# Weights loaded in pieces over the unit before, keys projected a block ahead, and the first layer's transposes on TensorE

## The chip, the cores and the metric

The kernel runs on the 8 cores of one Trainium2 chip. Every core works on one sequence of the batch, with the same weights, and the cores exchange nothing. The metric is the device time of the slowest core in microseconds.

## The reference: what is computed

A trunk of four pre-norm residual layers over a sequence of 16 meta tokens and 2048 tokens, model width 1024, branch width 2048. Layers 0 and 2 are pooling mixers, layers 1 and 3 are gated linear attention (GLA); a final RMSNorm follows, and the meta positions are dropped.

- Pooling layer: `u, z = split(h @ w_in)`. The 2048 channels of u fall into four groups of 512 with trailing windows of 2, 4, 8 and 16 tokens; from the mean over the window the token itself is subtracted, a 512 x 512 matrix of the group follows, then a channel scale and `silu(z)`, and `@ w_out` is added to h.
- GLA layer: four heads, key width 256, value width 512. `log_a = log_sigmoid(glr @ w_gate2 + b) / 16`, where `glr` is a projection of rank 16 of the normed input. Over chunks, with `cum` the running sum of `log_a`: `o = tril(qe ke^T) v + qe S` with `qe = q exp(cum)`, `ke = k exp(-cum)`, and the state `S = exp(g) S + kd^T v`. Then an RMSNorm per head, `silu(z)`, and `@ w_out` is added to h.

## The kernel before, in words

**Layout.** h stays in SBUF in float32 for the whole run (16 tiles of 128 tokens by 1024, and the meta tokens apart). The normed activations stand transposed in `hnT` (features on partitions, bfloat16). `BLOCKS` cuts the tokens into nine blocks: 144 tokens, seven of 256, 128 (two tiles of 128 in a block of 256).

**Units.** The work is 16 units: four groups per pooling layer (windows 8, 16, 4, 2 in this order) and four heads per GLA layer. Each unit goes over the nine blocks. A unit has four weight buffers, `W[0]` to `W[3]`, of 128 x 4096 bfloat16, in two sets (`Wt[0]`, `Wt[1]`) that alternate from unit to unit. `wload` (L462) fills one by a DMA from POOL's queue, which reads 2 MB of float32 and casts it. `load_unit(ui)` (L483) issues all loads of a unit; it is called at the end of a unit for the unit after the next (L719, L907), so each load waits on POOL's queue for the last reader of the buffer it fills.

**Pooling unit** (`pool_layer`, L605). `fold(ui)` (L506) multiplies the group matrix into the weights of u: 32 matmuls of 512 columns, in which ACT copies the results to `W[0]`. It is called in the unit before, after block 4 (for unit 0, at its own start), and behind it the output weights are loaded over the group matrix in `W[2]`. Per block: `zpart` and `upart` (32 matmuls each of the block's columns), `window` (prefix sums on POOL, then VectorE), `outp` (16 matmuls of 512 columns, added to h).

**GLA unit** (`gla_layer`, L731). Per block `proj` (L766) makes q, k, v and z, `gates` (L743) the decays of the next block, and `chunk` (L824) runs once per tile: scores, output, state update, output projection. The state update needs `kd`, which is `ke` transposed by a DMA from SP's queue (`xbar`, L407), issued in `proj` as soon as `ke` is written; there are two `kd` buffers. `glr_block` (L570) makes the rank-16 projection of a block from `hnT`, 8 matmuls, in the last unit of the pooling layer, right behind the block's `outp` (`after_block`, L593).

**Norms.** `norm_tile` (L552): ACT squares and sums (`rms`), VectorE scales into one of two buffers `hnb`, and a DMA transpose from SP's queue writes `hnT`. In layer 0 `norm_block` (L563) does so at the start of unit 0, two blocks ahead; later `after_tile` (L583) does it behind the last output projection of a tile.

**Order.** No order is written out. `Prog.schedule` (L109) takes all operations with their dependences and planned costs and simulates five in-order queues (PE, ACT, DVE, POOL, SP); whatever is ready first goes first, ties by the order of the program. The planned costs are constants: an operation of PE counts as ready 200 ns late (`PE_SLACK`), a VectorE operation costs `n/0.96 + 68` ns, one of POOL `1.7 n + 100` ns, a DMA 2200 ns and its bytes at 200 B/ns. DMAs have three planned channels (`bulk`, `x`, `tr`) that don't disturb each other in the plan. The result is a fixed order per queue, and `place` adds the semaphore waits. A DMA whose waits aren't met holds up everything behind it on the queue that issues it, ACT and POOL included: the loads of x are issued from ACT's queue (L916), each waiting for the one two before it.

**Start.** `load_first` (L470) loads the group matrix, the two halves of Wu (`W[3]`), then the z and the output weights of unit 0; `load_unit(1)` follows.

Of the kernel before, what the change touches and what calls it, by code (L numbers as in the profile page):

```python
# [41 lines left out]
class Prog:  # L42
# [3 lines left out]
    SEM = 120.0  # L46
    PE_SLACK = 200.0
    DMA_NS_PER_BYTE = 1.0 / 200.0
    DMA_FIX = 2200.0

    def __init__(self):
        self.ops = []
        self.dsems = {}

    def _touch(self, op, reads, writes):
# [227 lines left out]
def tile_col0(i):  # L283
    return 0 if i == 0 else NMETA + (i - 1) * 128
# [9 lines left out]
def build(n_layers=4):  # L294
# [60 lines left out]
    def carve(phase, name, nbytes, dtype, shape):  # L355
# [8 lines left out]
                 ("SA", 4352, F32, [128, 4, 272]), ("sg1", 2048, F32, [128, 2, 256]), ("U0", 4352, F32, [128, 4, 272]),  # L364
                 ("Y0", 2048, BF16, [128, 4, 256]), ("Y1", 2048, BF16, [128, 4, 256]), ("Y2", 2048, BF16, [128, 4, 256])]
    plan_gla = [("Eq", 2048, F32, [128, 2, 256]), ("Ek", 2048, F32, [128, 2, 256]),
                ("el0", 32, F32, [128, 2, 2]), ("el1", 32, F32, [128, 2, 2]), ("el2", 32, F32, [128, 2, 2]),
                ("qe0", 1024, BF16, [128, 2, 256]), ("ke0", 1024, BF16, [128, 2, 2, 128]),
# [6 lines left out]
                ("sz1", 2048, BF16, [128, 4, 256]),  # L375
                ("kd1", 512, BF16, [128, 256]), ("am1", 256, BF16, [128, 128]),
                ("S", 4096, F32, [128, 2, 512]), ("Sb", 2048, BF16, [128, 2, 512]),
# [17 lines left out]
    def mm(reads, writes, lst):  # L395
# [9 lines left out]
        P.op("pe", fn, reads, writes, dur, 170.0)  # L405

    def xbar(sem, out_, in_, reads, writes, nbytes):  # L407
        P.dma("sp", sem, lambda q: q.dma_start_transpose(out=out_, in_=in_), reads, writes, nbytes, chan="tr")  # L408
# [16 lines left out]
    def dve_dur(n):  # L425
        return n / 0.96 + 68.0

# [33 lines left out]

    def wload(ui, p, c0, c1, dst, name, part=None):  # L462
        s = ui % 2
        b = Wb[s][p] if part is None else part
        return dma("pool", name, dst, wpack[ui][:, c0:c1], [], [b], 128 * (c1 - c0) * 4)

# [15 lines left out]

    def load_unit(ui):  # L483
        if ui >= len(units):
            return
        li, u = units[ui]
        s = ui % 2
        W = Wt[s]
        if li % 2 == 0:
            wload(ui, 1, 4096, 8192, W[1][:], "W%d1" % s)  # L490
            wload(ui, 3, 12288, 16384, W[3][:], "W%d3" % s)
            wg_at[ui] = (W[2][:, 0:2048], Wb[s][2])
            dma("pool", "W%d2" % s, W[2][:, 0:2048], wpack[ui][:, 0:2048], [], [Wb[s][2]], 128 * 8192)
        else:
            for p in range(4):
                wload(ui, p, 4096 * p, 4096 * p + 4096, W[p][:], "W%d%d" % (s, p))

# [8 lines left out]
    def fold(ui):  # L506

        s = ui % 2
        W = Wt[s]
        wg, wgb = wg_at[ui]  # L510
        WuT = W[3][:, :].rearrange("p (fc n) -> p fc n", fc=4)
        wgv = wg.rearrange("p (fc n) -> p fc n", fc=4)
        for mt in range(8):
            b = proj_bank()
            mm([Wb[s][3], wgb] + ([b_wuh[mt // 4]] if ui == 0 else []), [bank[b]],
               [(PS[b][:, :], WuT[:, fc, mt * 128:(mt + 1) * 128], wgv[:, fc, :], fc == 0, fc == 3) for fc in range(4)])
            act([bank[b]], [Wb[s][0]], W[0][:, mt * 512:(mt + 1) * 512], PS[b][:, :], AF.Copy, psum=True)
        if ui != 0:
            wload(ui, 2, 8192, 12288, W[2][:], "W%d2" % s)

# [26 lines left out]
    def rms(i, k):  # L547
        act([hb[i]], [b_hnb[k], b_stat[i]], hnb[k][:, :], h[:, i - 1, :], AF.Square, accum=ssb[:, i:i + 1])
        act([b_stat[i], b_eps], [b_stat[i]], rstd[:, i:i + 1], ssb[:, i:i + 1], AF.Ln, scale=1.0 / D, bias=epsc[:, 0:1])
        act([b_stat[i]], [b_stat[i]], rstd[:, i:i + 1], rstd[:, i:i + 1], AF.Exp, scale=-0.5)  # L550

    def norm_tile(i):  # L552
# [39 lines left out]

    def after_block(li, bi):  # L593
        if li + 1 < n_layers and (li + 1) % 2 == 1:
            glr_block(bi, 4)

    orot = [0]
# [7 lines left out]
    def pool_layer(li, ui0):  # L605
# [3 lines left out]
        for gi in order:  # L609
# [7 lines left out]
            Wo = W[2][:, :].rearrange("p (oc n) -> p oc n", oc=4)  # L617
            for bi in range(NB):
                tiles, c0, n = BLOCKS[bi]
                if li == 0 and gi == 0:  # L620
# [77 lines left out]
                if ui == 0:  # L698
                    if bi == 0:
                        fold(0)  # L700
                    upart()
                    if bi == 0:
                        dma("pool", "cst2", tri[:], cst[:, 128:256], [], [b_tri], 65536, after=[xs[9]])
                        load_unit(1)
                    zpart()
# [25 lines left out]
    def gla_layer(li, ui0):  # L731
# [11 lines left out]
        def gates(k_):  # L743
            hd, bi = steps[k_]
            tiles, c0, n = BLOCKS[bi]
            el, b_el = T["el%d" % (k_ % 3)], A["el%d" % (k_ % 3)]
            offs = offs_of(bi)
# [17 lines left out]

        def proj(k_):  # L766
            hd, bi = steps[k_]
            ui = ui0 + hd
            s = ui % 2
# [3 lines left out]
            Wv = W[1][:, :].rearrange("p (kc n) -> p kc n", kc=8)  # L773
            Wz = W[2][:, :].rearrange("p (kc n) -> p kc n", kc=8)
            tiles, c0, n = BLOCKS[bi]
            par = k_ % 2
            rd = [hnTb[t_] for t_ in tiles]
            qe, ke, sz = T["qe%d" % par], T["ke%d" % par], T["sz%d" % par]
            b_qe, b_ke, b_sz = A["qe%d" % par], A["ke%d" % par], A["sz%d" % par]
            for dst, bd, Wm in ((qe, b_qe, Wq), (ke, b_ke, Wk)):  # L780
                b = proj_bank()
# [6 lines left out]
                else:  # L788
# [7 lines left out]
                    for k, (t_, o, m) in enumerate(offs_of(bi)):  # L796
                        if t_ < NT - 1:
                            kn = "kd%d" % (t_ % 2)
                            xbar(kn, T[kn][:, :].rearrange("p (f m) -> p f m", f=2), ke[:, k, :, :].rearrange("p f m -> p (f m)"),
                                 [b_ke], [A[kn]], 65536)  # L800
            for t_, o, m in offs_of(bi):
# [22 lines left out]
        def chunk(k_, k, t_, o, m):  # L824
# [5 lines left out]
            b_qe, b_ke, b_sz = A["qe%d" % par], A["ke%d" % par], A["sz%d" % par]  # L830
            el, b_el = T["el%d" % (k_ % 3)], A["el%d" % (k_ % 3)]
            vn = "vb%d" % (t_ % 3)
            vb = T[vn]
            cp = t_ % 2
            kdn, amn, yn, rn = "kd%d" % cp, "am%d" % cp, "yT%d" % cp, "rs%d" % cp
            kd, am, yT, rs = T[kdn], T[amn], T[yn], T[rn]
# [53 lines left out]

        nproj[0] = 3
        gates(0)
        for k_, (hd, bi) in enumerate(steps):
            ui = ui0 + hd
            proj(k_)
            if k_ + 1 < len(steps):
                gates(k_ + 1)
            for k, (t_, o, m) in enumerate(offs_of(bi)):
                chunk(k_, k, t_, o, m)
            if hd == 3:  # L900
                after_block(li, bi)
# [4 lines left out]
            if bi == NB - 1:  # L906
                load_unit(ui + 2)  # L907
                if hd < 2:
                    load_wg2(j, hd + 2)
# [90 lines left out]
```

How the kernel before makes its waits and increments, by code:

```python
        def replay(e, h):  # L233
            for waits, o in self.q[e]:
                for k, v in waits.items():
                    h.wait_ge(esem[k] if k in esem else dsem[k], v)
                ins = o.fn(h)
                if ins is None:
                    continue
                if o.sem is not None:
                    ins.then_inc(dsem[o.sem], 16)
                else:
                    ins.then_inc(esem[e], 1)
```

## Time and profile before

| | us |
|---|---|
| median of 3 runs | 2097.07 |
| lowest, highest | 2091.41, 2119.79 |
| profiled execution | 2109.36 |
| its span, slowest core (2) | 2107.8 |
| spans of the eight cores | 2047.6 to 2107.8 |
| PE busy on core 2 | 1899.1 |
| DVE, ACT, POOL busy | 1337.8, 1262.5, 441.9 |

All rows are of core 2 unless they say otherwise. PE is TensorE's matmuls, PEld its weight loads, which overlap them. Time is counted from the first instruction. `PEclk` is the clock that TensorE was granted in a stretch, 1.00 being 2.4 GHz and 0.50 1.2 GHz. A DMA has an issue on a queue (POOLq, SPq, ACTq) and a time to landing.

### The profile page before, as it was taken

How to read it: one execution, taken by the hardware profiler on the slowest of the kernel's cores; microseconds unless marked ns; L12 is line 12 of the kernel's file. 1: busy time of each engine (PE TensorE's matmuls, PEld its weight loads, DVE VectorE, ACT ScalarE, POOL GpSimd, SP SyncE). 2: the span in 40 equal slices, each digit the busy share in tenths (PEclk: the TensorE clock that was granted, in tenths of full speed). 3: DMA queues.
4: the chain of work that ended last, by engine and by line, in shares of the span. 5: the costliest groups of instructions: out<-in, count | busy, mean ns of one | idle time of the engine just before them, and what ended most of it. 6: DMA issues, size and time to landing. Idle time of an engine off the chain costs nothing.

```text
span 2107.8 us, 45126 instructions; the slowest of 8 cores (2047.6 to 2107.8 us)
## 1 busy us (share of the span) xinstructions
PE 1899.1 (90%) x15726; PEld 1353.8 (64%) x15944; DVE 1337.8 (63%) x2159; ACT 1262.5 (60%) x2711; POOL 441.9 (21%) x468
## 2 busy tenths in 40 slices
PE   1399989996998999999899998999799899899997
PEld 0267667774765766766566766777466576666765
DVE  0185555785775776777675556578466567677787
ACT  1365455564665665667675554556455566666786
POOL 1156683321000000000014667322000000000000
PEclk7699999998999999999999999999788899999999
DMA  9954122325004004022444221232500600500111
GB/s 166 121 115 78 30 42 41 67 48 105 10 10 87 9 15 83 9 43 42 75 69 55 51 41 31 41 71 46 100 7 8 86 9 10 88 9 9 39 70 75
DMA packets 121904, 111.15 MB, mean 53 GB/s; under 512 B 106944, under 2 KB 108880, under 8 KB 114640
## 3 DMA queue, kind: packets, MB, share of 16 engines
q0 software_dynamic: 11328, 63.49, 17.7%
q1 hardware_dynamic: 108048, 36.37, 9.4%
q10 hardware_dynamic: 2304, 8.39, 1.4%
q8 instruction: 130, 2.13, 0.4%
q14 instruction: 94, 0.77, 0.1%
HBM read 138.15 MB, written 8.39 MB: 70 GB/s over the span
## 4 chain that ended last, share of the span: by engine, by line
PE 71%; DMA 10%; issue 6%; DVE 5%; ACT 4%; POOL 3%; SPq 0%; ACTq 0%; DVEq 0%; POOLq 0%
PE ps L403 71%; DMA hnT<-hnb 6%; DMA kd<-ke 3%; POOL SA L434 2%; DVE hnb L429 1%; ACT sg L423 1%; POOL SB L434 1%; DVE Y L434 1%; ACT hnb L423 1%; DMA gbc<-gains 1%; DVE h L434 1%; DVE h L429 1%; ACT rstd L423 0%; ACT U L423 0%; SPq L408 0%
## 5 line engine op out<-in xcount | busy, mean ns | idle before, releaser
L403 PE MATMUL ps<-hnT,W 128*128 128x256 bf16 (+1 forms) x9216 | 994.5, 265 | 34.1 <-ACT U L423 28.3
L403 PEld LDWEIGHTS ps<-hnT,W 128*128 128x128 bf16 x9216 | 836.0, 99 | 184.2 <-issue 45.6
L429 DVE SCALAR_TENSOR_TENSOR h<-ps,rs,h 128x512 f32<-128x512 f32 x256 | 191.7, 749 | 132.0 <-ACT rs L423 59.8
L403 PE MATMUL ps<-W,Y 128*128 128x512 bf16 x957 | 240.8, 389 | 35.4 <-DVE Y L434 26.3
L403 PE MATMUL ps<-W,hnT 128*128 128x512 bf16 x1028 | 251.2, 386 | 6.6 <-DVE Eq L758 2.7
L434 DVE TENSOR_TENSOR h<-h,ps 128x512 f32<-128x512 f32 x256 | 175.2, 684 | 123.5 <-PE ps L403 121.9
L439 POOL COPY el<-Eq 128x2 f32<-128x2 f32 x136 | 27.5, 202 | 1013.5 <-ACT Eq L423 873.5
L403 PE MATMUL ps<-W,yT 128*128 128x512 bf16 x954 | 233.9, 385 | 4.4
L423 ACT ACTIVATE Sb<-S,el 128x512 bf16<-128x512 f32 x256 | 183.7, 717 | 65.5 <-DVE S L429 37.1
L429 DVE SCALAR_TENSOR_TENSOR S<-S,el,ps 128x512 f32<-128x512 f32 x240 | 178.4, 743 | 61.7 <-PE ps L403 47.5
L434 POOL TENSOR_TENSOR SA<-U 128x1080 f32<-128x1080 f32 (+7 forms) x72 | 134.8, 1872 | 332.6 <-ACT U L423 213.6
L423 ACT ACTIVATE U<-ps,vec 128x256 f32<-128x256 f32 (+2 forms) x288 | 129.2, 449 | 112.8 <-PE ps L403 86.4
L403 PEld LDWEIGHTS ps<-W,Y 128*128 128x128 bf16 x1024 | 98.9, 100 | 130.6 <-issue 43.9
L423 ACT ACTIVATE sg<-sg 128x512 f32<-128x512 f32 (+2 forms) x288 | 168.0, 585 | 21.6 <-ACT sg L423 1.1
L403 PEld LDWEIGHTS ps<-W,hnT 128*128 128x128 bf16 x1088 | 104.9, 99 | 110.6 <-issue 20.4
L423 ACT ACTIVATE gs<-gs 128x512 f32<-128x512 f32 (+2 forms) x288 | 168.0, 583 | 7.9 <-ACT gs L423 0.4
L429 DVE SCALAR_TENSOR_TENSOR hnb<-h,rstd,gbc 128x1024 bf16<-128x1024 f32 x64 | 105.5, 1649 | 102.3 <-ACT rstd L423 93.6
L423 ACT ACTIVATE hnb<-h 128x1024 bf16<-128x1024 f32 x80 | 84.3, 1054 | 138.1 <-DMA hnT<-hnb 85.7
L429 DVE SCALAR_TENSOR_TENSOR sz<-ps,vec,gs 128x256 bf16<-128x256 f32 (+2 forms) x288 | 129.9, 451 | 44.3 <-ACT gs L423 21.3
L403 PEld LDWEIGHTS ps<-W,yT 128*128 128x128 bf16 x1024 | 93.8, 98 | 94.6 <-issue 12.9
L434 DVE TENSOR_TENSOR Y<-ps,sg 128x512 bf16<-128x512 f32 (+1 forms) x144 | 90.9, 632 | 87.9 <-ACT sg L423 85.4
L423 ACT ACTIVATE sg<-ps 128x512 f32<-128x512 f32 (+1 forms) x144 | 78.5, 545 | 99.9 <-PE ps L403 99.8
(79 smaller groups left out, 2168.9 us busy)
## 6 DMA issues: line engine op xcount, KB each, us to landing
W<-wpack POOLq DMA_DIRECT2D x55, 1024.0 KB, 11.1
h<-x ACTq DMA_DIRECT2D x16, 512.0 KB, 4.8
out<-h SPq DMA_DIRECT2D x16, 512.0 KB, 2.7
W<-wpack POOLq DMA_DIRECT2D x10, 512.0 KB, 7.5
gbc<-gains SPq DMA_DIRECT2D x5, 512.0 KB, 6.6
kd<-ke SPq DMA_TRANSPOSE x128, 2.3
hnT<-hnb SPq DMA_TRANSPOSE x64, 3.1
Wglr<-wglrp POOLq DMA_DIRECT2D x2, 132.0 KB, 24.1
```

The source lines that it names most:

```text
L403: ins = e.matmul(o_, lhsT=l_, rhs=r_, start=st, stop=sp_)
L423: P.op("act", lambda e: e.activation(out=out_, in_=in_, func=func, scale=scale, **kw), reads, writes, dur, 130.0)
L429: P.op("dve", lambda e: e.scalar_tensor_tensor(out=out_, in0=a, scalar=s, in1=b, op0=op0, op1=op1), reads, writes, dve_dur(free_n(out_)) + ...
L434: P.op(eng, lambda e: e.tensor_tensor(out=out_, in0=a, in1=b, op=op), reads, writes, dve_dur(n) if eng == "dve" else n * 1.7 + 100.0, 100.0)
L439: P.op(eng, lambda e: e.tensor_copy(out=out_, in_=a), reads, writes, dve_dur(n) if eng == "dve" else n * 1.0 + 100.0, 100.0)
```

## The change

The loads of a unit are no longer issued in one go. `load_piece(ui, b, last_op)` issues one load (two in unit 0) of the next unit at blocks 0, 1, 5 and 6 (pooling) or 0, 2, 4 and 6 (GLA) of the current one, and makes it wait for the PE operation that the program named last (`P.last_pe`). `proj` is split: `proj_qk` makes k and then q of the block after the current one, `turn_k` issues the transposes of `ke` separately, with a third `kd` buffer and a fourth `el`, and `proj_vz` stays in its block. `gates` moves two blocks ahead. `norm_tile_pe` transposes by 8 TensorE transposes per tile into one PSUM bank and an ACT copy, and is used in `norm_block`, that is in layer 0 alone; an identity matrix is loaded for it ahead of the weights. `glr_block` runs one block later, and that of the last block after v and z of the GLA layer's first block. Three planned costs change.

```diff
-    PE_SLACK = 200.0
+    PE_SLACK = 400.0
...
+        if eng == "pe":
+            self.last_pe = op
...
+                 ("ident", 256, BF16, [128, 128])]
...
+("el3", 32, F32, [128, 2, 2]),
+("kd2", 512, BF16, [128, 256]),
...
     def dve_dur(n):
-        return n / 0.96 + 68.0
+        return n / 0.96 + 120.0
...
-             dve_dur(n) if eng == "dve" else n * 1.7 + 100.0, 100.0)
+             dve_dur(n) if eng == "dve" else n * 1.75 + 150.0, 100.0)
...
-    def load_unit(ui):
+    def load_piece(ui, b, last_op):
...
+        if units[ui][0] % 2 == 0:
+            if b == 0:
+                wload(ui, 3, 12288, 16384, W[3][:], "W%d3" % s, after=last_op)
+            elif b == 1:
+                wg_at[ui] = (W[2][:, 0:2048], Wb[s][2])
+                wload(ui, 2, 0, 2048, W[2][:, 0:2048], "W%d2" % s, after=last_op)
+            elif b == 5:
+                wload(ui, 1, 4096, 8192, W[1][:], "W%d1" % s, after=last_op)
+            elif b == 6:
+                wload(ui, 2, 8192, 12288, W[2][:], "W%d2" % s, after=last_op)
+        elif b % 2 == 0 and b < 8:
+            k = b // 2
+            wload(ui, k, 4096 * k, 4096 * k + 4096, W[k][:], "W%d%d" % (s, k), after=last_op)
...
+    def norm_tile_pe(i, b):
...
+        rms(i, k)
+        stt([hb[i], b_stat[i], b_gbc], [b_hnb[k]], hnb[k][:, :], h[:, i - 1, :], rstd[:, i:i + 1], gbc[:, :], ALU.mult, ALU.mult)
+        pT = PS[b][:, :].bitcast(BF16).rearrange("p (kc n) -> p kc n", kc=8)
+        tr([b_hnb[k], A["ident"]], [bank[b]], [(pT[:, kc, :], hnb[k][:, kc * 128:(kc + 1) * 128]) for kc in range(8)], T["ident"][:, :])
+        c0 = tile_col0(i)
+        act([bank[b]], [hnTb[i]], hnT[:, :, c0:c0 + 128], pT, AF.Copy, psum=True)
...
-                norm_tile(t_)
+                norm_tile_pe(t_, 4 + t_ % 2)
...
             for bi in range(NB):
+                if ui == 0:
+                    if bi == 3:
+                        dma("pool", "cst2", tri[:], cst[:, 128:256], [], [b_tri], 65536, after=[xs[12]])
+                    for b_ in {3: (0, 1), 5: (5,), 6: (6,)}.get(bi, ()) if units[1][0] % 2 == 0 else ():
+                        load_piece(1, b_, [P.last_pe])
+                else:
+                    load_piece(ui + 1, bi, [P.last_pe])
...
-                if gi == 3:
-                    after_block(li, bi)
+                if gi == 3 and bi > 0 and li + 1 < n_layers:
+                    glr_block(bi - 1, 4)
...
-            load_unit(ui + 2)
...
         gates(0)
+        proj_qk(0)
+        turn_k(0, 0)
+        turn_k(0, 1)
+        gates(1)
         for k_, (hd, bi) in enumerate(steps):
             ui = ui0 + hd
-            proj(k_)
+            load_piece(ui + 1, bi, [P.last_pe])
+            proj_vz(k_)
+            if k_ == 0:
+                glr_block(NB - 1, 4)
             if k_ + 1 < len(steps):
-                gates(k_ + 1)
+                proj_qk(k_ + 1)
+                turn_k(k_ + 1, 0)
+            if k_ + 2 < len(steps):
+                gates(k_ + 2)
             for k, (t_, o, m) in enumerate(offs_of(bi)):
                 chunk(k_, k, t_, o, m)
-            if hd == 3:
-                after_block(li, bi)
+                if k == 0 and k_ + 1 < len(steps):
+                    turn_k(k_ + 1, 1)
...
     load_gain(0)
+    dma("pool", "cst", T["ident"][:], cst[:, 0:128], [], [A["ident"]], 65536)
```

## Rows read from the trace of the kernel before

**Rows 1.** Cores: span and mean granted clock.
```profile
core 2: 2107.8 us, clock 0.951
core 4: 2073.8 us, clock 0.969
```
**Rows 2.** Stretches: length, busy us per engine (instructions), PEclk, DMA share, GB/s.
```profile
50.00:100.00 50.00, 13.47 (x76) 8.37 (x77) 5.68 (x4) 12.76 (x30) 3.43 (x5) 0.60 1.06 122
...
450.00:500.00 50.00, 36.61 (x310) 27.45 (x314) 34.32 (x37) 25.59 (x67) 11.29 (x9) 0.92 0.40 75
500.00:550.00 50.00, 43.30 (x359) 29.85 (x364) 28.08 (x58) 29.82 (x67) 2.23 (x8) 0.91 0.31 60
...
650.00:700.00 50.00, 40.87 (x351) 28.80 (x356) 26.00 (x53) 25.65 (x56) 1.28 (x5) 0.90 0.30 58
700.00:750.00 50.00, 49.69 (x408) 34.99 (x412) 36.79 (x67) 33.78 (x70) 1.12 (x6) 1.00 0.04 9
...
1530.00:1650.00 120.00, 118.89 (x812) 77.90 (x823) 73.82 (x131) 67.75 (x136) 2.48 (x13) 0.81 0.04 8
```
**Rows 3.** PE's waits: for what, us in total, times, longest.
```profile
PE ps L403 <- DMA kd<-ke: 32.2, 6, 8.8
PE ps L403 <- DMA hnT<-hnb: 28.9, 12, 7.8
```
**Rows 4.** The chain that ended last, pieces: start, us, what.
```profile
19.13 32.85 DMA hnT<-hnb
60.56 35.45 DMA hnT<-hnb
...
651.00 13.53 DMA kd<-ke
704.06 8.18 PE ps L403 x61
712.29 8.46 PE ps L403 x75
...
1594.74 9.83 PE ps L403 x61
1667.46 14.20 DMA kd<-ke
```
**Rows 5.** The timeline of PE at the start, and one of POOL.
```profile
21.55 5.08 PE L403 MATMUL ps<-W 128*128 128x512 bf16 x16
54.69 5.57 PE L403 MATMUL ps<-W 128*128 128x512 bf16 x16 [28.06 <-ACT W L423]
64.52 5.55 PE L403 MATMUL ps<-hnT,W 128*128 128x144 bf16 x48 [4.26 <-ACT rstd L423]
97.65 15.24 PE L403 MATMUL ps<-hnT,W 128*128 128x256 bf16 x128 [27.58 <-ACT U L423]
199.72 0.57 POOL L443 DMA_DIRECT2D W<-wpack  x1
```
**Rows 6.** Groups of instructions: count, busy us, mean ns, idle before.
```profile
L403 PE MATMUL ps<-hnT,W 128*128 128x128 bf16 x1024 | 65.3, 220 | 0.0
L423 ACT ACTIVATE hnb<-h 128x1024 bf16<-128x1024 f32 x9 | 9.5, 1051 | 7.6 <-DMA hnT<-hnb 7.6
```
**Rows 7.** Unit 0 from block 1 on, columns as in rows 2.
```profile
100.00:200.00 100.00, 94.99 (x776) 69.44 (x784) 70.17 (x82) 63.80 (x142) 58.37 (x41) 0.97 0.49 103
```
**Rows 8.** DMA issues of 480 to 486 us: count, size, median us to landing.
```profile
W<-wpack POOLq DMA_DIRECT2D x2, 1024.0 KB, 11.5
hnT<-hnb SPq DMA_TRANSPOSE x2, 14.0
```
**Rows 9.** DMA issues of the whole span.
```profile
h<-x ACTq DMA_DIRECT2D x16, 512.0 KB, 4.8
hnT<-hnb SPq DMA_TRANSPOSE x64, 3.1
```
**Rows 10.** POOL's waits.
```profile
POOL W L443 <- PE ps L403: 174.8, 38, 53.2
```

More of the change, by code:

```diff
@@ L53, in __init__ @@
         self.dsems = {}
+        self.last_pe = None
     def _touch(self, op, reads, writes):
@@ L375, in build @@
                 ("sz1", 2048, BF16, [128, 4, 256]),
-                ("kd1", 512, BF16, [128, 256]), ("am1", 256, BF16, [128, 128]),
+                ("kd1", 512, BF16, [128, 256]), ("kd2", 512, BF16, [128, 256]), ("am1", 256, BF16, [128, 128]),
                 ("S", 4096, F32, [128, 2, 512]), ("Sb", 2048, BF16, [128, 2, 512]),
@@ L405, in mm, with tr, fn @@
         P.op("pe", fn, reads, writes, dur, 170.0)
+    def tr(reads, writes, lst, idn):
+        def fn(e):
+            ins = None
+            for o_, i_ in lst:
+                ins = e.transpose(out=o_, in_=i_, identity=idn)
+            return ins
+        P.op("pe", fn, reads, writes, 57.0 * len(lst), 170.0)
     def xbar(sem, out_, in_, reads, writes, nbytes):
@@ L460, in build, with wload @@
     units = [(li, u) for li in range(n_layers) for u in (GROUPS if li % 2 == 0 else range(4))]
[L462 to L465, printed above, removed]
+    def wload(ui, p, c0, c1, dst, name, after=()):
+        return dma("pool", name, dst, wpack[ui][:, c0:c1], [], [Wb[ui % 2][p]], 128 * (c1 - c0) * 4, after=after)
     wg_at = {}
@@ L481, in load_first @@
         return o
-    def load_unit(ui):
+    def load_piece(ui, b, last_op):
         if ui >= len(units):
             return
-        li, u = units[ui]
         s = ui % 2
         W = Wt[s]
[L489 to L496, printed above, removed]
+        if units[ui][0] % 2 == 0:
[11 more added lines that the diff above has]
+            wload(ui, k, 4096 * k, 4096 * k + 4096, W[k][:], "W%d%d" % (s, k), after=last_op)
     rot = [0]
@@ L550, in rms @@
         act([b_stat[i]], [b_stat[i]], rstd[:, i:i + 1], rstd[:, i:i + 1], AF.Exp, scale=-0.5)
+    def norm_tile_pe(i, b):
+        k = nrot[0] % 2
+        nrot[0] += 1
+        rms(i, k)
[4 more added lines that the diff above has]
+        act([bank[b]], [hnTb[i]], hnT[:, :, c0:c0 + 128], pT, AF.Copy, psum=True)
     def norm_tile(i):
@@ L591, in after_tile @@
             final_tile(t_)
-    def after_block(li, bi):
-        if li + 1 < n_layers and (li + 1) % 2 == 1:
-            glr_block(bi, 4)
     orot = [0]
@@ L701, in pool_layer @@
                     upart()
-                    if bi == 0:
-                        dma("pool", "cst2", tri[:], cst[:, 128:256], [], [b_tri], 65536, after=[xs[9]])
-                        load_unit(1)
                     zpart()
@@ L745, in gates @@
             tiles, c0, n = BLOCKS[bi]
-            el, b_el = T["el%d" % (k_ % 3)], A["el%d" % (k_ % 3)]
+            el, b_el = T["el%d" % (k_ % 4)], A["el%d" % (k_ % 4)]
             offs = offs_of(bi)
@@ L764, in gates, with proj_qk @@
                 copy("pool", [A["Eq"]], [b_el], el[:, :, k:k + 1], Eq[:, :, o + m - 1:o + m])
-        def proj(k_):
+        def proj_qk(k_):
             hd, bi = steps[k_]
-            ui = ui0 + hd
-            s = ui % 2
+            s = (ui0 + hd) % 2
             W = Wt[s]
@@ L777, in proj @@
             rd = [hnTb[t_] for t_ in tiles]
-            qe, ke, sz = T["qe%d" % par], T["ke%d" % par], T["sz%d" % par]
-            b_qe, b_ke, b_sz = A["qe%d" % par], A["ke%d" % par], A["sz%d" % par]
-            for dst, bd, Wm in ((qe, b_qe, Wq), (ke, b_ke, Wk)):
+            qe, ke = T["qe%d" % par], T["ke%d" % par]
+            b_qe, b_ke = A["qe%d" % par], A["ke%d" % par]
+            for dst, bd, Wm in ((ke, b_ke, Wk), (qe, b_qe, Wq)):
                 b = proj_bank()
@@ L795, in proj, with turn_k, proj_vz @@
                             tt("dve", [bank[b], A["Ek"]], [bd], ke[:, k, :, :], pq[:, :, o:o + 128], Ek[:, :, o:o + 128], ALU.mult)
[L796 to L800, printed above, removed]
+        def turn_k(k_, k):
+            offs = offs_of(steps[k_][1])
+            if k < len(offs) and offs[k][0] < NT - 1:
+                kn = "kd%d" % (offs[k][0] % 3)
+                xbar(kn, T[kn][:, :].rearrange("p (f m) -> p f m", f=2), T["ke%d" % (k_ % 2)][:, k, :, :].rearrange("p f m -> p (f m)"),
+                     [A["ke%d" % (k_ % 2)]], [A[kn]], 65536)
+        def proj_vz(k_):
+            hd, bi = steps[k_]
+            s = (ui0 + hd) % 2
+            W = Wt[s]
+            Wv = W[1][:, :].rearrange("p (kc n) -> p kc n", kc=8)
+            Wz = W[2][:, :].rearrange("p (kc n) -> p kc n", kc=8)
+            tiles, c0, n = BLOCKS[bi]
+            rd = [hnTb[t_] for t_ in tiles]
+            sz, b_sz = T["sz%d" % (k_ % 2)], A["sz%d" % (k_ % 2)]
             for t_, o, m in offs_of(bi):
@@ L830, in chunk @@
             b_qe, b_ke, b_sz = A["qe%d" % par], A["ke%d" % par], A["sz%d" % par]
-            el, b_el = T["el%d" % (k_ % 3)], A["el%d" % (k_ % 3)]
+            el, b_el = T["el%d" % (k_ % 4)], A["el%d" % (k_ % 4)]
             vn = "vb%d" % (t_ % 3)
@@ L834, in chunk @@
             cp = t_ % 2
-            kdn, amn, yn, rn = "kd%d" % cp, "am%d" % cp, "yT%d" % cp, "rs%d" % cp
+            kdn, amn, yn, rn = "kd%d" % (t_ % 3), "am%d" % cp, "yT%d" % cp, "rs%d" % cp
             kd, am, yT, rs = T[kdn], T[amn], T[yn], T[rn]
@@ L905, in gla_layer @@
                 load_gain(min(li + 1, 4))
[L906 to L909, printed above, removed]
+            if bi == NB - 1 and hd < 2:
+                load_wg2(j, hd + 2)
     load_gain(0)
+    dma("pool", "cst", T["ident"][:], cst[:, 0:128], [], [A["ident"]], 65536)
     dma("sp", "meta", hmf, metaT[:, :], [], [hb[0]], 65536)
```

8 lines of the change are left out of this document (2 added, 6 removed).

## The prediction

> **What bounds the kernel now.** I read the cores first, then the stretches of 50 us, then what ended PE's waits, then the timeline of the start.
>
> The slowest core is core 2, at 2107.8 us [rows 1]; the others reach down to 2047.6. In the stretches, look for 49.7 of 50 us of PE at PEclk 1.00: 700 to 750 is one [rows 2], and there is nothing to win in it, because matmuls follow each other without a wait and a GLA block of 256 tokens takes 8.18 + 8.46 us [rows 4]. What can be won is in the stretches that fall out of this pattern, and each costs twice: PE idles, and then works at half clock for a while. I count the idle time as the lower end of a loss, and idle plus (1 - PEclk) x 50 as the upper end, since part of the slow time is idle itself.
>
> Three places stand out. At the **start**, 50 to 100 has 13.5 us of PE work at clock 0.60 [rows 2]. The chain shows why: two DMA transposes of `hnT` took 32.85 and 35.45 us [rows 4], where the median of all 64 is 3.1 [rows 9]. They sat behind weight loads. PE waited 28.06 us for an ACT copy of the fold and 27.58 us for an ACT write of U [rows 5]; both times ACT stood in order behind a square that needed an `hnb` buffer, which the transpose held. At the **pooling-to-GLA transitions**, 450 to 550 has 13.4 + 6.7 us idle at clock 0.92 and 0.91 [rows 2]; PE's waits for `hnT` transposes add to 28.9 us [rows 3]. Two weight loads had been issued with them: 11.5 us to landing, and the transposes took 14.0 [rows 8]. At the **unit boundaries of GLA** PE waits 32.2 us for `kd`, in six waits [rows 3]; the transposes behind them take 13.53 and 14.20 us in the chain [rows 4].
>
> A fourth loss is not a wait: from 1530 to 1650 PE is busy 118.9 of 120 us at clock 0.81 [rows 2]. Not every core has it: core 4's mean clock is 0.969 against core 2's 0.951 [rows 1].
>
> **The start.** The change removes 16 DMA transposes from SP's queue and adds 128 TensorE transposes and 16 ACT copies. It also takes the loads of unit 1 away from the first 60 us. The first half of the fold runs from 21.55 to 26.6 [rows 5]; its 16 matmuls then need no `hnT`. Without the 28.06 us wait the second half (5.57 us) ends at 32.2. I keep the 4.26 us between fold and block 0 [rows 5] for the last weight copies, so block 0 (5.55 us) ends at 42.0. Block 1 started at 97.65 before: 55.6 us earlier. From there to the end of the unit (a load that waits for its last output projection is issued at 199.72 [rows 5]) the work is the same but for the transposes. A matmul of 128 columns costs 65.3 / 1024 = 64 ns of PE [rows 6]; 128 of them make 8.2 us. Gain 55.6 - 8.2 = **47 us**. The x loads don't set the pace: two are in flight, so 4.8 / 2 = 2.4 us per tile [rows 9], and PE needs half a block of work for a tile, over 4 us. The lower bound: all 16 copies fall on the path, at 1.05 us each like an ACT pass over 128 x 1024 [rows 6], 17 us, and tiles 4 and 5 come 5 us late beside the weights of unit 0; 47 - 22 = 25. ACT is busy only 63.8 of 100 us in this unit [rows 7], so I take none of it. The upper bound: the 4.26 us go and the transposes fill idle time; 47 + 4 + 8 = 59.
>
> The row gives 64 ns per transpose as PE's share. The Trainium skill (TensorE: Matmul & The Clock Gate, "Part 4: PE-mode transpose") speaks against this edit: about 275 ns per 128 x 128 transpose inside a kernel. By that, 128 x 275 ns would be 35 us instead of 8.2 and the start's gain an estimated 20 us. The trace of before has no TensorE transpose to decide it.
>
> **kd.** Before, `turn` is issued when PE has only v and z of the same block left, and a landing of 13.53 us made PE wait 8.8. Now k is made a block ahead: 8.18 + 8.46 = 16.6 us of PE work [rows 4] lie between issue and use, more than the longest landing in the chain, 14.20. The third `kd` buffer is what lets the first tile's transpose go early; the second tile's waits for one chunk. The cover is gone if two loads are in flight again, and the pieces are two blocks apart. So the 32.2 us go, with the slow clock behind them: 650 to 700 loses 9.1 idle and at most 9.1 + 5.0 with the clock [rows 2], a factor up to 1.55, that is 32 to 50 us. I take **40**, and 20 as the low end, if half of the waits come back.
>
> **Rank projection.** 28.9 us of waits [rows 3], and by 450 to 550 up to 4.0 + 4.5 us of clock per transition; with half of the clock for two transitions 37 us. Block 7's projection now has all of block 8 before it. What is late next is block 8's own: its tile is normed some 4 us after its output projection, and v and z of a block of 144 tokens, k, q and gates, about half of 16.6 us, cover 8 to 9 us. But the first piece of the next unit's weights waits for the gates and so is issued just then; with a landing like the 14.0 us of [rows 8] PE waits up to 9 us, without it none. I take 4 to 5 per transition: gain **28**, bounds 10 and 46.
>
> **Costed at nothing.** The same bytes of weights go over POOL's queue. Each piece waits for a PE operation of the block before, and behind it on POOL stand the window sums of a pooling unit, or the `el` copies of GLA. Before, loads waited 174.8 us on POOL for PE [rows 10] and POOL had room; the sums feed an output projection one block or more away. If this cover is gone, each wait of POOL is a wait of PE. On SP, 16 `hnT` transposes go and the `kd` ones stand earlier, in order with the norms' in the last head. On ACT the x triggers no longer stand behind squares. The identity load puts Wg 0.6 us later (one POOL issue takes 0.57 [rows 5]). Wu, Wg and z weights of a pooling unit get three blocks of lead, 30 us for a landing of 11.5 [rows 8]. The three planned costs reorder everything slightly: -10 to +10 us, taken as 0.
>
> **Sum.** The profiled execution took 2109.36 us (span 2107.8), 12.3 above the median. 2109.4 - 47 - 40 - 28 = 1994; less 12 on the scale of the median, **1982 us**. Low gains (25 + 20 + 10) give 2042, high ones (59 + 50 + 46) 1942; 10 us of order on the good side give 1932. The 0.81 stretch is kept as it is.
>
> **Rivals.**
>
> *A, slower: the clock at 0.81 spreads.* PE without pauses could draw the lower clock for longer. Place: both GLA layers, some 590 us each; price: 9.83 against 8.18 us for the same 61 matmuls [rows 4], 20%. Lower in both and throughout, less the 120 us that have it already: 1982 + 0.20 x (1180 - 120) = 2194. It decides once over (2139 - 1982) / 0.20 = 785 us more are slow, and makes the time slower by over 2%. For: the stretch that has it is one without a pause, and it held for 120 us. Against: 700 to 750 has no pause and 1.00 [rows 2], and core 4 shows by its mean clock that the stretch is not the program's alone [rows 1]. Chance 0.06. Only through the last layer: 1982 + 0.20 x (590 - 120) = 2076, no change; chance 0.06.
>
> The Trainium skill (same page, "Part 1: The HAM clock gate", on the peak-current limiter) has 13/16 of the clock as soon as three cores of a die run dense matmuls, for as long as they do. That would be A. This case's trace disagrees: in the dense stretch of 700 to 750 core 2 has 1.00.
>
> *B, the paced loads stall.* POOL is held by pieces waiting for a late PE, and window sums behind them come late. Place: 32 pieces in the pooling units; at 3 us each 96 us, 1982 + 96 = 2078, no change. For: 174.8 us of such waits [rows 10]. Against: POOL was idle in them. Chance 0.05.
>
> *C, the start is paid back.* ACT and late x tiles eat 22 us: 2004. Chance 0.11.
>
> *The change doesn't do what it says:* transposes of `kd` still issue late because the planner, which gives them 2.2 us plus bytes, puts the k projection just ahead of its chunk. Then kd's 40 stay: 2022; I count it within the forecast's range.
>
> **How the numbers follow.** Forecast 0.72, C 0.11, A 0.12 in its two sizes, B 0.05. A difference within 2% is about what a measurement of this kernel can't tell from none. Faster by more, below 2055: forecast and C, 0.83. Within: B and the smaller A, 0.11. Slower: the larger A, 0.06. The range holds the forecast with its bounds and C, 1930 to 2045.
>
> **What would show it.** First PE block 1 near 42 us instead of 97.65, and no wait of tens of us on ACT; the transposes at some 64 ns each. Waits of PE for `kd` near 0 and for `hnT` under 10. At unit boundaries 49.7 of 50 at 1.00. Wrong, if a pooling unit shows PE waiting for VectorE's Y behind late POOL sums, if unit 0 ends after 175, or if PEclk is 0.81 in stretches that had 1.00.

## The result, and the profile after

The changed kernel takes 2008.87 us and the kernel before 2094.24 (medians of four executions each). The ratio is 0.9581, 95% interval 0.9481 to 0.968: 4% faster. The forecast was 1982 with 1930 to 2045. The profiled execution took 2008.14 us against 2109.36, 101 us less; the forecast on that scale was 115 less. Executions in which the cores of a die are held at a lower clock are left out of all ratios, and of the times that I quote for the experiments.

The cores after, and below them the stretches of the slowest one, core 3 (columns as in [rows 2]):

```profile
core 1: 1978.1 us, clock 0.988
core 2: 2000.6 us, clock 0.975
core 3: 2006.5 us, clock 0.973
core 4: 1979.3 us, clock 0.989
```
```profile
0.00:50.00 50.00, 18.40 (x124) 12.18 (x125) 9.18 (x14) 20.85 (x43) 5.69 (x14) 0.90 0.91 186
50.00:100.00 50.00, 46.81 (x438) 36.07 (x436) 39.97 (x41) 42.05 (x92) 35.84 (x23) 1.00 0.41 99
...
400.00:450.00 50.00, 42.15 (x311) 29.84 (x310) 30.21 (x36) 26.23 (x63) 9.02 (x8) 0.81 0.49 79
450.00:500.00 50.00, 45.35 (x333) 29.73 (x332) 27.26 (x56) 28.59 (x63) 2.57 (x10) 0.79 0.31 61
500.00:550.00 50.00, 50.00 (x344) 32.61 (x343) 31.21 (x55) 30.36 (x60) 1.27 (x5) 0.81 0.15 28
650.00:700.00 50.00, 50.00 (x415) 35.00 (x413) 35.48 (x66) 34.54 (x70) 2.17 (x8) 1.00 0.27 50
700.00:750.00 50.00, 50.00 (x470) 36.23 (x468) 35.15 (x68) 35.41 (x76) 2.36 (x9) 1.00 0.16 29
```

Three things are to be seen. From 50 to 100 PE works 46.8 us at full clock where it worked 13.5 at 0.60 [rows 2]. From 650 to 700, where a unit boundary stood, nothing is lost any more. And the transition from pooling to GLA, now at 400 to 500, still has 7.9 + 4.7 us idle. The stretch at 0.81 now lies here, on cores 2 and 3; before, it lay at about 1500 to 1650, on cores 2, 3, 6 and 7. Core 1 hasn't got it and ends 28 us before core 3.

PE's waits on core 3, as in [rows 3]:

```profile
PE ps L415 <- DVE msq L446: 18.5, 1, 18.5
PE ps L407 <- DVE Y L446: 18.4, 21, 3.2
PE ps L407 <- DMA hnT<-hnb: 15.7, 4, 6.6
PE ps L415 <- DVE hnb L441: 9.7, 3, 8.3
PE ps L407 <- ACT Eq L435: 7.4, 2, 4.5
PE ps L407 <- DVE yT L446: 5.1, 5, 2.1
PE ps L407 <- DVE qe L441: 3.6, 2, 1.9
```

The first row is the time until PE's first instruction; before, that was 21.1 us. The 32.2 us for `kd` [rows 3] are gone without a rest, and so are the two waits of 28 us at the start [rows 5]. The waits for `hnT` are only halved. Those for the gates' chain (`Eq` holds the decays, `qe` the queries times them) have grown to 11.0 us, from 2.9 before, and those for the pooling output `Y` have fallen. The two rows of the kernel before, core 2:

```profile
PE ps L403 <- DVE Y L434: 27.2, 16, 4.5
...
PE ps L403 <- DVE Eq L758: 2.9, 6, 0.6
```

The timeline of PE at the start, and at the end of unit 0:

```profile
24.70 9.24 PE L407 MATMUL ps<-W 128*128 128x512 bf16 x32
42.24 1.01 PE L415 MATMUL ps<-ident,hnb 128*128 128x128 bf16 x8 [8.29 <-DVE hnb L441]
45.09 2.08 PE L407 MATMUL ps<-hnT,W 128*128 128x144 bf16 x16 [1.84 <-ACT W L435]
...
53.86 1.91 PE L407 MATMUL ps<-hnT,W 128*128 128x256 bf16 x16
...
157.44 1.89 PE L407 MATMUL ps<-W,Y 128*128 128x512 bf16 x8
```

The fold runs through without the pause of before, block 1 starts at 53.9 instead of 97.65, and unit 0 ends at 159.3 instead of 199.7 [rows 5]. Block 1 was forecast near 42. The 8.29 us of idle time come from ACT:

```profile
38.18 0.33 ACTq L455 DMA_DIRECT2D h<-x  x1
38.87 1.06 ACT L435 ACTIVATE hnb<-h 128x1024 bf16<-128x1024 f32 x1 [7.63 <-DMA h<-x]
```

The trigger of an x tile waits for the one two before it, which lands late beside the weights of unit 0, and ACT's queue stands behind it.

Core 2 before and core 3 after are one core each. On all eight cores, unit 0 (counted to the last weight load of its output projection) ended between 172 and 199 us before, 186.5 on average, and ends between 156 and 162 now, 158.8 on average. So the start is 40 us shorter from slowest core to slowest core, and 28 on average; core 2 was the latest of the eight.

### The profile page after: what moved, and what is told of

Its sections match the earlier page's. It is cut to its first block, busy times and chain, and to the rows that moved or that the text cites. A ratio compares the mean times of both kernels' runs of the same rounds, so it can differ in the third digit from the quotient of the medians.

```text
span 2006.5 us, 45600 instructions; the slowest of 8 cores (1978.1 to 2006.5 us)
## 1 busy us (share of the span) xinstructions
PE 1907.1 (95%) x16072; PEld 1357.0 (68%) x16072; DVE 1323.1 (66%) x2159; ACT 1293.4 (64%) x2727; POOL 447.6 (22%) x469
## 4 chain that ended last, share of the span: by engine, by line
PE 79%; DVE 5%; issue 5%; POOL 4%; DMA 4%; ACT 3%; ACTq 0%; DVEq 0%; SPq 0%; POOLq 0%
PE ps L407 79%; DMA hnT<-hnb 3%; POOL SA L446 2%; POOL SB L446 2%; DVE Y L446 1%; DVE hnb L441 1%; DMA gbc<-gains 1%; DMA h<-x 1%; ACT hnb L435 1%; DVE Eq L780 0%; ACT Eq L435 0%; POOL U L451 0%; DVE h L446 0%; ACT sg L435 0%; DVE S L441 0%
## 5 line engine op out<-in xcount | busy, mean ns | idle before, releaser
L407 PE MATMUL ps<-hnT,W 128*128 128x256 bf16 (+1 forms) x9216 | 984.1, 264 | 9.5 <-DVE qe L441 3.6
L407 PE MATMUL ps<-W,Y 128*128 128x512 bf16 x1024 | 250.8, 387 | 16.9 <-DVE Y L446 15.1
L407 PE MATMUL ps<-W,hnT 128*128 128x512 bf16 x1088 | 261.7, 385 | 0.0
L407 PE MATMUL ps<-W,yT 128*128 128x512 bf16 x1024 | 245.8, 382 | 0.4 <-DVE S L441 0.4
L446 POOL TENSOR_TENSOR SA<-U 128x1080 f32<-128x1080 f32 (+7 forms) x72 | 140.5, 1952 | 322.5 <-ACT U L435 251.1
L435 ACT ACTIVATE gs<-gs 128x512 f32<-128x512 f32 (+2 forms) x288 | 168.4, 586 | 15.1 <-ACT gs L435 0.7
L435 ACT ACTIVATE Eq<-ps,nbias 128x256 f32<-128x256 f32 (+1 forms) x144 | 65.2, 453 | 145.8 <-DVE qe L441 112.0
L441 DVE SCALAR_TENSOR_TENSOR hnb<-h,rstd,gbc 128x1024 bf16<-128x1024 f32 x64 | 98.3, 1537 | 65.1 <-ACT rstd L435 55.0
```

The lines of the kernel that those rows point to most:

```text
L407: ins = e.matmul(o_, lhsT=l_, rhs=r_, start=st, stop=sp_)
L435: P.op("act", lambda e: e.activation(out=out_, in_=in_, func=func, scale=scale, **kw), reads, writes, dur, 130.0)
L441: P.op("dve", lambda e: e.scalar_tensor_tensor(out=out_, in0=a, scalar=s, in1=b, op0=op0, op1=op1), reads, writes, dve_dur(free_n(out_)) + ...
```

## The experiments

Each ratio is against the kernel before in the experiment's own session (medians 2088 to 2096 us). Times are to be held against 2094 (before) and 1990, the changed kernel in the one execution in which every core has a mean clock of 0.985 or more (spans 1978 to 1989 us); in all twelve profiles of the experiments no core had the stretch at 0.81. That 1990 is a single execution of another session, so a difference of some 10 us counts here only where the spans of the single cores show it too. Expectations that start from 2009 have the 0.81 stretch in them.

**1. The transposes of layer 0 back to DMA.**

```diff
-                norm_tile_pe(t_, 4 + t_ % 2)
+                norm_tile(t_)
```


> The changed kernel with the first layer's transposes back as DMA transposes; all else stays. Theory: the start's gain is theirs, since a DMA transpose lands only when the weight loads in flight have landed; without the loads of unit 1 in the first 60 us only the first of the two long landings of before (33 and 35 us) comes back, so PE waits about 25 us more at the start and the time is 2009 + 25 = 2034. Rival, that the start was freed by the pacing, as unit 1's loads no longer stand ahead: 2009 within 8.

Ratio 0.9677 (0.9608 to 0.9745), 2012 and 2025 us: 22 and 35 worse than the changed kernel. As the theory had it, one long wait for the fold's copies comes back, 15.7 to 21.2 us on the eight cores, and unit 0 ends between 167 and 193 us, 177.5 on average. Core 1:

```profile
51.98 6.19 PE L407 MATMUL ps<-W 128*128 128x512 bf16 x16 [21.17 <-ACT W L435]
```

**2. The loads in one go again.** All loads of a unit are issued at the end of the unit two before it (those of unit 1 in unit 0), without `after`; the output weights go behind the fold.

```diff
-                    load_piece(ui + 1, bi, [P.last_pe])   # pooling; GLA likewise
+            load_piece(ui + 2, 0, ())   # after the unit's blocks: all loads
...
+        if ui != 0:   # end of fold
+            wload(ui, 2, 8192, 12288, W[2][:], "W%d2" % s)
```

> The changed kernel with each unit's loads issued together at the end of the unit before the last, as in the kernel before; keys ahead, rank projection and TensorE transposes stay. Theory: projecting the keys ahead is enough for the kd waits (0 to 5 us of PE's waits, against 32.2 before), and pacing brings nothing there; it even moves weight loads under the transposes of the last pooling unit. Time 2000 to 2015, that is the same as the changed kernel. Rival, that pacing removed the kd waits: 20 to 30 us of them come back, with the clock 2040 to 2050.

Ratio 0.9601 (0.9569 to 0.9634), 2003 us: the theory's figure. No core waits for `kd`: the lead of a block covers the trains, that is, loads issued right behind each other. The 13 us against 1990 are at the start, where unit 1's loads stand before the x tiles: unit 0 ends at 172.3 us on average instead of 158.8. The waits for `hnT` are longer too (PE's timeline, then its waits), but all that lies behind unit 0 takes no longer than in the changed kernel:

```profile
56.28 2.08 PE L407 MATMUL ps<-hnT,W 128*128 128x144 bf16 x16 [12.51 <-ACT W L435]
```
```profile
PE ps L407 <- DMA hnT<-hnb: 24.8, 5, 8.6
```

**3. Keys in their own block again.**

```diff
-                proj_qk(k_ + 1)
-                turn_k(k_ + 1, 0)
+            proj_qk(k_); turn_k(k_, 0); turn_k(k_, 1)   # ahead of proj_vz(k_)
...
-                gates(k_ + 2)
+                gates(k_ + 1)
```


> The changed kernel with q and k projected in their own block again and the transposes of ke right behind them; pacing and the rest stay. Theory: pacing alone spreads the collisions over the unit, four single loads of 9 to 10 us each instead of one train; PE waits up to 4 us for kd at each of some 30 loads in the GLA units, 60 to 100 us with the clock, so 2070 to 2110, no better than the kernel before. Rival, that single loads are short enough for the old lead: kd waits under 10 us and 2009 to 2020.

Ratio 0.9526 (0.9494 to 0.9558), 1987 us: my theory fell. The rival's `kd` waits under 10 us came; its 2009 to 2020 us was counted from 2009, and against 1990 the time is even 3 us lower. The longest `kd` wait on any core is this one:

```profile
PE ps L407 <- DMA kd<-ke: 0.7, 1, 0.7
```

A single load is short enough for the old lead. Projecting the keys ahead (experiment 2) and pacing the loads, that is, issuing them in pieces, each remove the `kd` waits by themselves; beside pacing the first is worth nothing that the runs can tell.

**4. The kernel before with the TensorE transposes alone.**

```diff
-                norm_tile(t_)
+                norm_tile_pe(t_, 4 + t_ % 2)
...
+    dma("pool", "cst", T["ident"][:], cst[:, 0:128], [], [A["ident"]], 65536)
```

> The kernel before with the TensorE transposes in layer 0 alone. Theory: it takes the 28 and 28 us waits of PE at the start away and leaves all others: 2094 - 45 = 2050 (2040 to 2060). Rival, that loads of unit 1 and 2, which are still issued in the first 62 us, now hold up the x tiles instead of the transposes: gain under 20 us, 2075 to 2094.

Ratio 0.9936 (0.9894 to 0.9979), 13 us: the rival. Unit 0 ends at 170.4 us on average, 16 earlier. The long wait is now an x trigger's, and the loads still come in trains (PE's timeline, then its waits, on core 2, the slowest; on the others the `kd` waits are 18 to 40 us):

```profile
56.20 2.08 PE L404 MATMUL ps<-hnT,W 128*128 128x144 bf16 x16 [12.70 <-ACT W L432]
```
```profile
PE ps L404 <- DMA kd<-ke: 56.7, 6, 15.4
PE ps L404 <- DMA hnT<-hnb: 32.6, 10, 10.0
```

**5. The rank projection undelayed.**

```diff
-                if gi == 3 and bi > 0 and li + 1 < n_layers:
-                    glr_block(bi - 1, 4)
+                if gi == 3 and li + 1 < n_layers:
+                    glr_block(bi, 4)
...
-            if k_ == 0:
-                glr_block(NB - 1, 4)
```


> The changed kernel with the rank projection of a block right behind its output projection again, the last one included. Reference: 1990 us, the changed kernel on cores whose clock stays at 1.00 or 0.50. Theory: the delay by a block is worth what it hides, and the piece loads, issued in the same moment as a block's transposes, make the need larger than in the kernel before: PE's waits for hnT rise from 15.7 us to 35 or more and the time by 20 to 30, to 2010 to 2020. Rival, that the delay hides nothing that the pieces don't take back: 1990 within 6.

Ratio 0.9472 (0.9427 to 0.9517), 1980 us: 10 better, against both the theory and the rival. In the profiles its cores end between 1964 and 1978; those of the changed kernel without the 0.81 stretch between 1978 and 1986. `hnT` waits are shorter, not longer (core 0, where the changed kernel has 16.5; two short `kd` waits are new):

```profile
PE ps L407 <- DMA kd<-ke: 7.5, 2, 4.2
PE ps L407 <- DMA hnT<-hnb: 6.4, 5, 3.0
```

**6. The rank projection three blocks late.**

```diff
-                if gi == 3 and bi > 0 and li + 1 < n_layers:
-                    glr_block(bi - 1, 4)
+                if gi == 3 and bi > 2 and li + 1 < n_layers:
+                    glr_block(bi - 3, 4)
...
-            if k_ == 0:
-                glr_block(NB - 1, 4)
+            if 1 <= k_ <= 3:
+                glr_block(NB - 4 + k_, 4)
```


> The changed kernel with the rank projection three blocks late instead of one: blocks 0 to 5 in the last pooling unit, 6 to 8 in the first GLA unit. Theory: the 28 us that the prediction gave to this part were missed because the transposes of hnT stand behind a piece load issued with them, by 7 to 11 us, and a block is not enough cover; with three blocks PE's waits for hnT go from 15.7 us to 0 and the time by 15 to 20, to 1970 to 1976. Rival, that PE waits next for the gates' chain (ACT and DVE at the start of the GLA layer, 11 us already): under 6 us gained, 1984 to 1990.

Ratio 0.9522 (0.9476 to 0.9568), 1990 us, which is the rival's figure for another reason than the rival's. Six of eight cores end at 1970 to 1979 without a wait for `hnT`, as the theory had it. Cores 2 and 4 lose some 15 us in one place, the last pooling unit of the first layer. On core 4 two pieces, issued 8 us apart, met two transposes there (DMA issues of 374 to 383 us; the figures are medians of two, the loads alone took 10.9 and 24.4):

```profile
W<-wpack POOLq DMA_DIRECT2D x2, 1024.0 KB, 17.7
hnT<-hnb SPq DMA_TRANSPOSE x2, 21.4
```

**7. The x loads from SP's queue,** from the fourth tile on.

```diff
-        return dma("act", "x%d" % i, ...
+        return dma("act" if i < 4 else "sp", "x%d" % i, ...
```


> The changed kernel with the loads of x from the fourth tile on issued from SP's queue instead of ACT's. Theory: of the 38 us still lost at the start 8 are a wait of ACT for the landing of an x tile, at the trigger of a later one, in front of the fold's copies; without it the fold goes on and the time falls by 6 to 10, to 1980 to 1984. Rival, that the x tiles themselves are late beside the weights of unit 0 (13 to 15 us to landing): under 3 us, 1987 to 1990.

Ratio 0.9519 (0.9446 to 0.9591), 1990 us: the rival. PE still waits 6.60 and 6.20 us at the start, for tiles that land late: ACT now waits for a tile at the square that reads it (5.93 and 4.30 us), again in front of the fold's copies. Whose queue issues the loads doesn't matter.

**8. The old planned costs.**

```diff
-    PE_SLACK = 400.0
+    PE_SLACK = 200.0
-        return n / 0.96 + 120.0
+        return n / 0.96 + 68.0
-             dve_dur(n) if eng == "dve" else n * 1.75 + 150.0, 100.0)
+             dve_dur(n) if eng == "dve" else n * 1.7 + 100.0, 100.0)
```


> The changed kernel with the three old planned costs. Theory, as predicted: a slightly different order, worth between -10 and +10 us and probably nothing: 1984 to 1996. Rival: the 200 ns more of slack and the dearer VectorE are what took 6 us of PE's waits for Y out of the pooling units; without them 1997 to 2010.

Ratio 0.9494 (0.9439 to 0.955), 1983 to 1987 us: within the 10 us that I had given to the order. But this small sum hides a gain and a loss: with the old costs the two transitions (last pooling unit and first GLA unit together) are 5 and 8.5 us shorter on average and PE waits 4 to 7 us for `hnT` instead of 12 to 17, and more than half of that is lost again elsewhere. So the new order has a part in the transitions' time too.

**9. The kernel before with pacing alone.**

```diff
-            load_unit(ui + 2)
+                    load_piece(ui + 1, bi, [P.last_pe])   # each block, pooling
...
+            load_piece(ui + 1, bi, [P.last_pe])           # each step, GLA
             proj(k_)
```

> The kernel before with the loads paced as in the changed kernel, and nothing else: DMA transposes in layer 0, q before k in their own block, two kd buffers, rank projection at once, old planned costs. Theory after the first runs: pacing is the part that carries the gain, because single loads no longer queue in trains before the transposes; kd waits fall from 32.2 us to under 10 and the time to 2000 to 2020, three quarters of the whole gain. Rival, that pacing needs k made ahead of q, which the variant without keys ahead still had: kd waits stay above 20 us and the time at 2040 or more.

Ratio 0.9673 (0.96 to 0.9747), 2012 to 2039 us, the theory's figure by the median (2019): 3.3% of the whole change's 4.2% by the ratios, or 75 of 104 us if the changed kernel is taken at 1990. Unit 0 ends at 170.2 us on average, 16 earlier than before, although its transposes are the DMA's. On the slowest core of the profile:

```profile
PE ps L406 <- DMA hnT<-hnb: 38.4, 9, 17.7
...
PE ps L406 <- DMA kd<-ke: 3.6, 2, 2.6
```

**10. The kernel before with pacing and TensorE transposes.** The edits of 4 and 9 together:

```diff
-                norm_tile(t_)
+                norm_tile_pe(t_, 4 + t_ % 2)
...
-            load_unit(ui + 2)
+                    load_piece(ui + 1, bi, [P.last_pe])
```

> The kernel before with pacing and the TensorE transposes, without keys ahead, delayed rank projection and new planned costs. Theory: these two parts are the whole change, at the start each frees what the other leaves; 1975 to 1990, the changed kernel or up to 10 us better, since undoing the rank projection's delay gained 10. Rival, that the parts left out are worth something together, as keys ahead with the old lead cover the pieces: 2000 to 2030.

Ratio 0.963 (0.9574 to 0.9686), 2008 to 2019 us: the rival's range, but not for the rival's reason, as no core waits more than 4.4 us for `kd`. The start does what the theory said: unit 0 ends at 161.9 us on average. Cores 3, 4 and 6 end at 1987 to 1988, as the theory had it; but in each execution some cores end 15 to 30 us later, in the profiled one because of a transition, and the slowest one counts. Core 5 at its transition, the DMA issues of 449 to 457 us and the wait that follows, and then the same place on core 1:

```profile
W<-wpack POOLq DMA_DIRECT2D x2, 1024.0 KB, 21.4
hnT<-hnb SPq DMA_TRANSPOSE x2, 25.6
```
```profile
489.32 1.89 PE L407 MATMUL ps<-hnT,Wglr 128*66 128x256 bf16 x8 [29.96 <-DMA hnT<-hnb]
```
```profile
W<-wpack POOLq DMA_DIRECT2D x2, 1024.0 KB, 9.0
hnT<-hnb SPq DMA_TRANSPOSE x2, 8.7
```

The same four transfers, the loads 7 us apart, take two to three times as long on one core as on the other (core 5's loads 10.2 and 32.7 us, its transposes 16.6 and 34.5).

**11. The undelayed projection, with the pieces moved.** In the last pooling unit all four pieces at blocks 0 and 1, in the first GLA unit at blocks 1, 3, 5, 7.

```diff
-                    load_piece(ui + 1, bi, [P.last_pe])                # pooling
+                    for b_ in ((0, 2, 4, 6)[2 * bi:2 * bi + 2] if gi == 3 and bi < 2 and li + 1 < n_layers else (bi,) if gi < 3 else ()):
+                        load_piece(ui + 1, b_, [P.last_pe])
-            load_piece(ui + 1, bi, [P.last_pe])                        # GLA
+            load_piece(ui + 1, bi - (hd == 0), [P.last_pe])
```
and the edit of 5.

> The changed kernel with the rank projection undelayed, and the pieces moved off the transposes around the pooling-to-GLA transition: all four of the last pooling unit at its blocks 0 and 1, those of the first GLA unit at blocks 1, 3, 5 and 7. Reference: the undelayed variant, 1980, with PE's waits for hnT of 12.3 us. Theory: what is left of those waits is the collision of a piece with the transposes issued in the same moment; they fall under 5 us and the time by 8 to 14, to 1966 to 1972. Rival, that PE waits for the norm's chain itself: 1977 to 1983.

Ratio 0.9426 (0.9359 to 0.9492), 1970 us, the theory's figure, though `hnT` waits of 4 to 11 us remain, against the theory's under 5; the longest is now at block 0, where the four pieces stand.

**12. The late projection, with the pieces apart.**

```diff
-                    load_piece(ui + 1, bi, [P.last_pe])                # pooling
+                    load_piece(ui + 1, bi - (gi == 3), [P.last_pe])
-            load_piece(ui + 1, bi, [P.last_pe])                        # GLA
+            load_piece(ui + 1, bi - (hd == 0), [P.last_pe])
```
and the edit of 6.

> The changed kernel with the rank projection three blocks late, and the pieces issued in the last pooling unit and in the first GLA unit one block later, at blocks 1, 3, 5 and 7, so that no piece falls within a block or two of another. Reference: 1990 for the late projection alone, which has a core with a wait of 15 to 20 us for transposes that stood under two overlapping loads, and 1970 for the moved pieces alone. Theory: two loads in flight with a transpose waiting is what costs 15 to 20 us at a time; with loads apart and three blocks of cover PE's waits for hnT are under 3 us on every core and the time is 1960 to 1968. Rival, that such waits come back elsewhere or the gates' chain takes their place: 1972 to 1990.

Ratio 0.9379 (0.9339 to 0.9419), 1962 to 1965 us: the theory's figure, and the fastest of all. No core waits more than 0.6 us for `hnT`, and none shows a wait for `kd`. Yet the transposes still stand under pieces: at the transition of core 2 two of them take 10.1 and 9.5 us. What hides them is the three blocks of cover, and no two pieces overlap there. Its slowest core at the transition reads:

```profile
400.00:450.00 50.00, 44.97 (x363) 31.85 (x361) 39.63 (x48) 31.58 (x79) 9.30 (x8) 0.97 0.50 83
450.00:500.00 50.00, 47.96 (x431) 34.67 (x430) 34.98 (x70) 35.90 (x79) 2.06 (x9) 1.00 0.31 56
```

## Why the prediction was right, and which step was not

**The start: right, 40 us for 47, on the cores compared.** Unit 0 ends 199.7 - 159.3 = 40 us earlier. Block 1 starts 43.8 us earlier, not the 55.6 forecast. What the lower bound had named came true in part: the x tiles are late beside unit 0's weights and cost 8.3 us. The sum had let the x loads set no pace, by their median of 4.8 us over the whole span [rows 9]; the fourth and fifth took 13.0 and 15.1 us here. That the term came so near is in part luck of the core, as the average over the cores is 28. The ACT copies cost next to nothing: from block 1 to the end of the unit 105 us pass instead of 102, transposes included. The transposes took

```profile
L415 PE MATMUL ps<-ident,hnb 128*128 128x128 bf16 x128 | 11.7, 247 | 30.3 <-DVE msq L446 18.5 <-DVE hnb L441 9.7 <-ACT rsm L435 2.1
```

11.7 / 128 = 91 ns of PE each, not the 64 that I took. The 275 ns of the Trainium skill (TensorE: Matmul & The Clock Gate, "Part 4: PE-mode transpose") is near the 247 ns that one lasts here; as they overlap, it is no price for a row of them.

But I gave the gain to the transposes, and experiments 1, 4, 9 and 10 show that it belongs to two parts. By the average end of unit 0, the TensorE transposes alone bring 16 us of it (13 in all), pacing alone 16 as well, since it takes unit 1's loads out of the start, and both together 25 of the 28. That pacing belongs to the start I had in a half sentence and in no term.

**kd: right in size, wrong in its reason.** The waits went to 0, and with them the slow clock at the boundaries. On cores without the 0.81 stretch the two GLA layers took 597 and 573 us before and take 572 and 561 now: 37 us less, where 40 were forecast. I had made the lead of a block the cause; experiments 2, 3 and 9 show that either part does it, and that pacing does without the other: with pacing alone the two layers take 568 and 557 us. The two pooling layers behind unit 0, which no term names, are 8 us shorter each on these cores (302 to 294 and 396 to 388).

**Rank projection: the step that failed.** 28 us were forecast for it. PE's waits for `hnT` fell from 28.9 to 15.7 us, 13 less, and those for the gates' chain grew from 2.9 to 11.0, 8 more: about 5 are left, and experiment 5 shows that the delay itself costs 10. The step said that block 7's projection "now has all of block 8 before it", and looked for a collision at block 8 alone. The pieces collide earlier. Each waits for the PE operation that the program named last: in the last pooling unit that is the delayed rank projection just behind a block's output projection, so the piece goes out while that block is being normed. In the first GLA unit the first piece waits for the gates, as the prediction had it. In the chain of the changed kernel, three transposes of the transition stand under a piece:

```profile
398.72 9.66 DMA hnT<-hnb
...
432.37 7.68 DMA hnT<-hnb
...
453.03 9.84 DMA hnT<-hnb
```

A piece had been issued at 396.3 (10.2 us to landing); PE waited 6.6 us for the transpose, until 408.6. So pacing did not take the loads away from the transposes at the one place where PE needs these soon. Experiment 12, which keeps the pieces apart and gives the projection three blocks, brings 27 us (1990 to 1963), and all of it there: the last pooling unit and the first GLA unit together take 250 to 255 us in the changed kernel on cores without the 0.81 stretch, and 237 to 242 in experiment 12, at both transitions. Why the delayed order is slower than the undelayed one I haven't isolated. Undelayed, a piece waits for the block's own rank projection, and so for that block's transposes; but the planner orders everything else anew as well, and experiment 8 shows that the order alone moves the two transitions by 5 and 8.5 us.

**The rivals.** B, pieces that hold POOL up, did not come: POOL waits longer for PE before its loads (280.2 us against 174.8 [rows 10]), but PE's waits for `Y` fell from 27.2 to 18.4 us. C came in part, with 8.3 of its 22 us. A did not come: a stretch of some 150 us at 0.81 is in this profile, on two cores, as in that of before, on four, and the changed kernel has 50.00 of 50 us of PE at 1.00 from 650 to 700 and from 700 to 750. The rule of the Trainium skill (same page, "Part 1: The HAM clock gate") that three cores with dense matmuls take a die to 13/16 does not describe these profiles: the changed kernel has the stretch on two cores of a die only, and in all twelve profiles of the experiments no core shows it, though all eight run the same dense matmuls.

## What to carry to other kernels

A DMA transpose on which TensorE waits must be kept clear in time of bulk loads, or be given work enough to cover it (three blocks here); look at what event releases each of them, since a load that waits for "the end of the block" starts with that block's transposes. When two edits can each remove a wait, test each alone: here one of them brought 3.3 of 4.2%. On eight cores the slowest counts, so a collision that happens on one core in four is paid in full.

## What the runs showed of the hardware

- A DMA transpose issued under one weight load of 1 MB lands shortly after the load does (9.7 us under a load of 10.2, where alone it takes 3.1; in the profile after, 0.6 to 3.2 us behind the load).
- With a second load in flight it may go much worse. In experiment 10 the two loads took 9.0 us (median) on core 1 and 21.4 on core 5, the transposes 8.7 and 25.6, by the same program. The 35.45 us at the start of the kernel before [rows 4] have this form too: two loads behind a transpose, 27.6 and 33.3 us to landing. What decides between the two cases is open. At the transitions of experiments 6, 9 and 10, wherever a second piece was issued with transposes waiting, it took 18.9 to 32.7 us in the seven cases in which the first had 2.5 to 3.1 us to go, and at most 10.5 us where it had 2.3 or less. Elsewhere in experiments 9 and 10 overlaps of up to 10.8 us went without such a collapse, so the overlap alone doesn't decide.
- The stretch at 0.81 comes once in a profile that has it, lasts some 150 us and begins near a pooling-to-GLA transition: between 1485 and 1501 us before, at 416 and 417 after. The cores that have it after end at 2000.6 and 2006.5 us, the others of that die at 1985.8 and 1978.1. What makes it come or go the runs don't show: it is missing in all twelve profiles of the experiments, but these were taken in other sessions.
